# The seam between a recurrence and a dense unit: outputs split in two, products taken kind by kind, two weight sums moved

## What is computed

```python
h = rms_norm(x, norm_w) * (1 + scale) + shift          # from the conditioning vector
proj = h @ w_in                                        # 1024 x 6656
attn = sliding_window_attention(aq, ak, av, sinks) * silu(ag)
f = lb + (1 - lb) * sigmoid(rf)
rec = rms_norm(hgrn2_chunkwise(rq, f, ri), rec_norm_w) * silu(rg)
out = x + gate * (concat(attn, rec) @ w_out)
# hgrn2: b = cumsum(log f) in a chunk; q_dec = q*exp(b); k_inv = k*exp(-b)
# out = tril(q_dec k_inv^T) v  +  q_dec S      (rows' part + states' part)
# S   = decay * S + k_out^T v
```

## Time and profile before

| | us |
|---|---|
| three timed runs | 1797.95, 1798.18, 1799.14 (median 1798.18) |
| the profiled execution, its span | 1796.91, 1795.1 |
| busy PE / DVE / ACT / POOL | 1761.7 / 1284.5 / 975.0 / 476.2 |
| granted clock of PE | 0.999 of full speed |

### The profile page before, as it was taken

The page is one execution under the profiler, slowest core; times in us unless marked ns, Lnnn a source line. Parts: engine busy times, 40 slices in busy tenths (PEclk is TensorE's granted clock), DMA queues, the critical chain, the costliest instruction groups (busy, mean ns, idle before and its releaser), DMA issues.

```text
span 1795.1 us, 28444 instructions
## 1 busy us (share of the span) xinstructions
PE 1761.7 (98%) x9882; PEld 1505.8 (84%) x9882; DVE 1284.5 (72%) x2628; ACT 975.0 (54%) x2127; POOL 476.2 (27%) x825
## 2 busy tenths in 40 slices
PE   6999999999999999999999999999999999999998
PEld 4788888999978888878888899998888888888887
DVE  7965476777767676697546677776776567987986
ACT  5622224888876665562222578888655565343441
POOL 1000025777722122210002576772222220000000
PEclk9999999999999999999999999999999999999999
DMA  9242332222123354344233222121433158178242
GB/s 362 71 164 92 120 106 101 75 71 75 52 93 98 119 147 130 111 160 164 80 119 112 104 72 80 43 85 50 168 97 98 53 168 320 64 255 301 101 175 94
DMA packets 158494, 222.30 MB, mean 124 GB/s; under 512 B 11792, under 2 KB 104336, under 8 KB 150672
## 3 DMA queue, kind: packets, MB, share of 16 engines
q1 hardware_dynamic: 158352, 220.49, 36.4%
HBM read 163.18 MB, written 57.28 MB: 123 GB/s over the span
## 4 chain that ended last, share of the span: by engine, by line
PE 88%; DVE 4%; DMA 2%; ACT 2%; issue 2%; POOL 2%; SPq 0%; POOLq 0%; ACTq 0%; DVEq 0%
PE bank L924 69%; PE bank L1114 3%; PE bank L1100 3%; PE bank L1084 3%; PE bank L1209 1%; PE bank L1189 1%; PE bank L1224 1%; PE bank L1185 1%; DMA x_home<-in_x 1%; DMA h_f<-x_cols 1%; PE bank L1035 1%; PE bank L1237 1%; PE bank L1214 1%; DVE g_lo L1923 0%; ACT sm L1552 0%
## 5 line engine op out<-in xcount | busy, mean ns | idle before, releaser
L924 PE MATMUL bank<-h_hi,w_hi 128*128 128x512 f32 x512 | 206.5, 403 | 0.2
L924 PE MATMUL bank<-h_lo,w_hi 128*128 128x512 f32 x512 | 199.9, 390 | 0.0
L924 PE MATMUL bank<-h_hi,w_lo 128*128 128x512 f32 x512 | 199.7, 390 | 0.0
L924 PE MATMUL bank<-wq_hi,h_hi 128*128 128x384 f32 x512 | 179.6, 351 | 0.5 <-issue 0.5
L924 PE MATMUL bank<-ob_hi,oa_hi 128*128 128x512 f32 x448 | 175.0, 391 | 0.2 <-DVE ob_lo L2364 0.2
L924 PE MATMUL bank<-ob_hi,oa_lo 128*128 128x512 f32 x448 | 174.4, 389 | 0.0
L924 PE MATMUL bank<-ob_lo,oa_hi 128*128 128x512 f32 x448 | 174.3, 389 | 0.0
L924 PE MATMUL bank<-wq_hi,h_lo 128*128 128x384 f32 x512 | 172.1, 336 | 0.0
L924 PE MATMUL bank<-wq_lo,h_hi 128*128 128x384 f32 x512 | 171.4, 335 | 0.0
L1406 ACT ACTIVATE g_hi<-g_raw 128x2048 fp32r<-128x2048 f32 x36 | 69.0, 1916 | 162.3 <-PE bank L924 155.8
L1552 ACT ACTIVATE sm<-sm,neg_m 128x257 f32<-128x257 f32 x256 | 127.6, 501 | 6.5 <-DVE neg_m L2170 1.4
(11 more groups left out here) (258 smaller groups left out, 4670.9 us busy)
## 6 DMA issues: line engine op xcount, KB each, us to landing
g_raw<-in_w_in SPq DMA_DIRECT2D x24, 1024.0 KB, 6.1
raw<-in_w_in SPq DMA_DIRECT2D x16, 1024.0 KB, 7.9
o_lower<-mixed_cols SPq DMA_DIRECT2D x32, 512.0 KB, 6.3
nat_rows<-u SPq DMA_DIRECT2D x48, 256.0 KB, 2.6
raw<-in_w_in SPq DMA_DIRECT2D x8, 1536.0 KB, 6.7
o_upper<-in_w_out SPq DMA_DIRECT2D x24, 512.0 KB, 8.1
wa<-in_w_ada SPq DMA_DIRECT2D x8, 1024.0 KB, 11.3
g_q<-gate_cols SPq DMA_DIRECT2D x64, 128.0 KB, 2.8
```

The source lines that it names most:

```text
L924: mm = pe.matmul(dst, a, b, start=(first and m == 0), stop=(last and m == 2), **more)
```

## The change

In the last step of recurrence 0 (t = 16) PE does the rows' part of the outputs, then scores and turned keys, group 1 of product 0, and only then the states' part; group 3 of product 0 goes ahead of the transposes and outputs of step 17. ACT makes its squares behind the copy of the turned keys, and all four copies of product 0 right behind the rounding of B21, ahead of the modulation of A21. Unit 3 gets a function of its own on PE: products 1, 2, 3, 4 and 6 are issued by halves (groups 0 and 1, then 2 and 3), and in a half kind by kind over the four depths, each kind with its own wait; product 5 stays as it was. The transposes of the last rows go behind the whole of product 1. On DVE the low part of B11' (product 2) goes ahead of the last rows, and T4 goes from between the additions of product 3 to behind the combination of group 1 of product 4. SP and POOL are not edited.

```diff
+            HH, HL, LH = (0, 0), (0, 1), (1, 0)
+            def kind(n, e, which, cs, ks=range(KH), first=False, last=False):
+                at, operand = PRODUCTS[e]
+                h, w = which
+                for k in ks:
+                    for c in cs:
+                        mm = pe.matmul(ring(n, at + c)[:, :], operand(k)[h][:, tokens(c)],
+                                       (g_hi, g_lo)[w][w_slot(n, e)][:, k, :], start=(first and k == 0),
+                                       stop=(last and k == KH - 1), skip_group_check=True)
+                        if last and k == KH - 1:
+                            mm.then_inc(blk_ok, 1)
+            def by_kinds(n, e, cs):
+                at = (PRODS + 1) * (n // GU) + e + 2
+                pe.wait_ge(whi_ok, PRODS * n + e + 1)
+                pe.wait_ge(hhi_ok, at)
+                kind(n, e, HH, cs, first=(e != 1))
+                for which in ((HL, LH) if e == 2 else (LH, HL)):
+                    if which == HL:
+                        pe.wait_ge(wlo_ok, PRODS * n + e + 1)
+                    else:
+                        pe.wait_ge(hop_ok, at)
+                    kind(n, e, which, cs, last=(which == (LH if e == 2 else HL)))
+            def first_unit(n):
+                s, halves = n // GU, ((0, 1), (2, 3))
+                if s > 0:
+                    for cs in halves:
+                        pe.wait_ge(p1_ok, 4 * n + cs[1] + 1)
+                        by_kinds(n, 1, cs)
+                    mix_transposes(s - 1, REC_T - 1)
+                for cs in halves:
+                    if s > 0 and cs[0] == 0:
+                        pe.wait_ge(rmix_ok, QB * s * REC_T)
+                    elif s > 0:
+                        pe.wait_ge(ot_ok, s * REC_T)
+                    by_kinds(n, 2, cs)
+                for cs in halves:
+                    pe.wait_ge(c11_ok, 4 * n + cs[1] + 1)
+                    by_kinds(n, 3, cs)
+                for cs in halves:
+                    pe.wait_ge(comb_ok, comb(n, COMB_U2, cs[1]))
+                    by_kinds(n, 4, cs)
+                for c in range(4):
+                    pe.wait_ge(comb_ok, comb(n, COMB_22, c))
+                    strassen(n, s, 5, c)
+                for cs in halves:
+                    pe.wait_ge(comb_ok, comb(n, COMB_U3, cs[1]))
+                    by_kinds(n, 6, cs)
             def gemm_p1(s, u, c):
...
                 n = s * GU + u
+                if n in (GU,):
+                    first_unit(n)
+                    return
                 if u > 0:
...
+                output_rows(T, t)
+                output_states(T, t)
+            def output_rows(T, t):
                 b = t % 2
...
                               skip_group_check=True)
+            def output_states(T, t):
+                b = t % 2
                 pe.wait_ge(st_ok, STEPS * (T + 1))
...
                         break
+                    if t == REC_T + 1:
+                        gemm_p1(s + 1, 0, 3)
                     if t >= 3:
                         mix_transposes(s, t - 3)
-                    if t >= 2:
+                    if t == REC_T:
+                        output_rows(T - 2, t - 2)
+                    elif t >= 2:
                         outputs(T - 2, t - 2)
...
                         chunk_products(s, T - 1, t - 1)
-                    if t == REC_T and s + 1 < SEGS:
+                    if t == REC_T:
                         gemm_p1(s + 1, 0, 1)
+                        output_states(T - 2, t - 2)
                     if 1 <= t <= REC_T:
...
                         transpose_half(half)
-                    if s + 1 < SEGS and t >= REC_T - 1:
-                        gemm_p1(s + 1, 0, (0, 2, 3)[t - (REC_T - 1)])
+                    if s + 1 < SEGS and REC_T - 1 <= t <= REC_T:
+                        gemm_p1(s + 1, 0, (0, 2)[t - (REC_T - 1)])
...
                         forget_tanh(s, t)
-                    if s + 1 < SEGS and t == REC_T + 1:
-                        for c in range(3):
-                            copy_p1(s + 1, GU * (s + 1), c)
                     if t >= 3 and not (s + 1 == SEGS and t == REC_T):
                         mix_copy(s, t - 3)
-                    if s + 1 < SEGS and t == REC_T:
-                        mix_squares(s, t)
                     if t < REC_T:
...
                     if s + 1 < SEGS and t == REC_T:
+                        mix_squares(s, t)
                         hi_a12(s + 1)
                         weights_hi(GU * (s + 1), 1)
+                        for c in range(4):
+                            copy_p1(s + 1, GU * (s + 1), c)
                         modulate_a21(s + 1)
...
                         if t == REC_T + 1:
-                            copy_p1(s + 1, GU * (s + 1), 3)
                             weights_hi(GU * (s + 1), 2)
...
                 if n == GU:
+                    weights_lo(n, 2)
                     mix_rows(s - 1, REC_T + 1)
-                    weights_lo(n, 2)
                 else:
...
                 add_u2(1)
-                weights_t4(n)
+                if n not in (GU,):
+                    weights_t4(n)
                 add_u2(2)
...
                     dve.tensor_tensor(c22[c % 3][:], ring(n, 4 + c)[:, :], u3[c][:], ALU.add).then_inc(comb_ok, 1)
+                    if n in (GU,) and c == 1:
+                        weights_t4(n)
                 if u == 0:
```

## The result

The changed kernel's median is 1800.66 us (1797.51 to 1804.93, 22 runs), that of the kernel before beside it 1798.2 us (1795.81 to 1800.79, 22 runs): ratio 1.0013, 95% interval 1.0007 to 1.0019. So it is slower by 2.3 us (1.3 to 3.4), less than 0.2%. Predicted: 1799.9, within 0.2%.

The account below looks back on a forecast made before the run. PE bounds the kernel (busy 1761.7 of 1795.1 us), with DVE next. Waits closed -3.3, products 3 and 4 late +2.0, store +3.0 give +1.7 us: median 1799.9 us, range 1795.4 to 1802.6, no change within 0.2%.

Parts of the forecast that it names:

- Part 1: Recurrence 0's last step: PE's 2.7 us wait at the states' part goes; group 2 waits for the masked copy, 2.3 us earlier.
- Part 2: ACT and last rows: r_mix ready at about 787.4 instead of 785.2; product 2 starts at 787.9 against 791.20, 3.3 us gained.
- Part 3: Products 3 and 4: ACT's later meeting and DVE's chain cost 2.0 us; product 4 starts at 811.6, 1.3 us gain left.
- Part 4: T4 moved: the c22 store lands at 832.9 behind two loads; PE stalls 3.0 us before product 5's group 3.
- my own sign: Start of product 4: if it comes by 810.3, the step on products 3 and 4 being late is wrong.
- Rival (a): Product 5: the c22 store doesn't hold group 3; -1.3 us, 1796.9 us; chance 0.18.
- rival (b): Products 3 and 4: DVE's chain isn't the bound either, all 3.3 to 3.7 us are kept; 1794.7 us; chance 0.12.
- Rival (c): Product 5: the store lands later than 835 us, PE stalls 7.7 us; +6.4 us, 1804.6 us; chance 0.12.
- Rival (d): Step 16: scores wait for k_inv or the masked copy comes later; 1 to 2 us less gain, 1801.2 us; chance 0.08.

Follow-up runs that it names:

- store_first: Changed kernel with SP storing c22 of groups 0 and 1 before it waits for T4 and issues the two 1 MB loads; ratio 0.9984 to the kernel before.
- act_store: Changed kernel with the store of c22 of group 0 issued by ACT on its own DMA queue after T4; ratio 1.0011 to the kernel before.
- one_load: Changed kernel with SP issuing only one of the two loads ahead of the store of c22 of group 0; ratio 0.999 to the kernel before.
- fill_wait: Changed kernel with 12 more matmuls, results unused, on PE ahead of product 5's last group; ratio 1.0003 to the kernel before.
- t4_alone: Kernel before with only T4 moved behind the combination of group 1; ratio 1.0026 to the kernel before.
- t4_back_mask: Changed kernel with T4 in its old place and the masked copy of the scores right behind the state carries on DVE; ratio 0.9987 to the kernel before.
- kinds_only: Kernel before with unit 3 by halves and kinds and B11' low part ahead of the last rows; recurrence, ACT, T4 as before; ratio 1.0001 to before.
- t4_back: Changed kernel with T4 back in its old place between the additions of product 3; ratio 0.9983 to the kernel before.

## Why the prediction was right

The forecast (+1.7 us, no change by 0.2%, a touch slow) holds with +2.3 (1.3 to 3.4). Step by step:

- **Part 1, right in kind.** The states' part waits no more, group 2 waits for the masked copy, as named. I put 0.3 to 0.5 us; it is 0.19 us in the profiles of store_first, act_store, one_load and fill_wait, but 1.51 in the changed kernel's. There the load of rg_w for step 15 took 5.4 us to land where it was 2.8 before. DVE's scaling was held until 767.54 and the copy stands behind it. This load took 2.7 to 3.1 us in eight of the other profiles, 4.4 in t4_alone and 4.7 in t4_back_mask, and no edit lies ahead of it, so I take the late one for chance; how often it comes is not shown.
- **Part 2, one term off.** r_mix wasn't pushed back by POOL: the power started at 783.58 just ahead of S1 (783.61) and took 1.01 us, where it had taken 3.03 starting behind S1. r_mix started right behind the low part of B11', 1 us earlier after S1 than I had it. That the one behind waits stands: in kinds_only the power, 0.07 us behind S1, took 3.09 us, in the other runs it came first and took 1.01.
- **Part 3, sign right, size too big.** I had 2.0 us lost to ACT's meeting and DVE's chain. ACT did wait for the meeting, but it came 4.4 us after the last transposes (790.48 to 794.92) and not 6.0, because the last rows' store now lands in 2.9 us and not 4.4: B22's load is 2.65 us ahead of it (789.18, 791.83) instead of 1.4. The other runs agree: issued 1.4 to 1.6 us behind that load the store takes 4.1 to 4.4 us, 2.1 behind it 3.6 to 3.9, 2.65 behind it about 3.0, and 5.1 behind it 2.3 (kinds_only). With r_mix 1 us earlier too, product 4 of store_first starts at 810.20, 49.24 us after the transposes, 2.8 less than before's 52.05:

```profile
810.20 2.14 PE L970 MATMUL bank<-g_hi,h_hi 128*128 128x512 f32 x8
```

So of 3.3 us only 0.5 is lost, and by my own sign (product 4 by 810.3) the size of this step is wrong. The bound is still DVE's sum u2: t4_back's trace names it as what product 4 waits for (0.20 us). In the changed kernel's profile the late masked copy took 1.3 of the gain, and so product 4's start agreed with my sum (1.45 against 1.36 earlier) by an accident.
- **Part 4, the step that decides, right.** The store lands 9.2 us after T4 (8.3 predicted), PE's wait is 3.50 us in the trace and the group is 3.66 late (830.7 and 3.0 predicted, on my clock). store_first, t4_back and t4_alone show that nothing else carries the loss. What I gave as its cause, order within SP's ring, is only half of it: in act_store another queue didn't help.
- **Not foreseen:** the half clock behind the wait, 1.3 us in the changed kernel (4.18 us for 2.85); my sum has no term for it.

So two misses of opposite sign met: 1.5 us too much for part 3, 2.0 too little for part 4. The mechanism that decides was right, but that the time came within 0.6 us of the forecast is luck. With +0.5 for part 3 and 3.7 + 1.3 for part 4 the sum is -3.3 + 0.5 + 5.0 = +2.2 us, against the measured 2.3. Rival (a), a store that doesn't hold anything, is what store_first makes true, and the gain is then 2.9 us, nearer to rival (b) than to the 1.3 that I gave to it. Rival (c) with its 7.7 us stall didn't come: the second load took 8.0 us to land, near the 7.1 that I used and not the 12.0 of that rival. Rival (d), a masked copy that comes later still, did come in the profiled execution, at 1.3 us, and in none of the other profiles.

## What to carry to other kernels

When an operation is moved later on one engine, read the queue that waits for it: whatever stands behind that wait in the queue's order moves too, and here a 256 KB store that freed a buffer was caught behind 2 MB of loads. A small transfer that someone will wait for goes ahead of the loads on the same queue; another queue didn't save it here. And a wait closed at one place is worth little while the next engine's work isn't let in by finer waits: the split and the order kind by kind gained nothing that the time shows alone, and 2.0 us of the seam together (2.6 with T4 moved and the store first).

## What the runs showed of the hardware

- Behind PE's waits of 3.50 us (changed), 3.19 us (t4_alone) and 3.04 us (act_store) the granted clock fell to the 1.2 GHz level for some 2.8 us (about 3.3 in act_store): 0.50 in 835.8 to 838.6 of the changed kernel. In act_store it fell only 1.0 us after PE had started again, as its timeline shows (a later matmul of a row is some 0.39 us long at full clock, as in the earlier trace rows, 0.63 at the lower). Behind the 2.68 us of the kernel before it stayed at 1.00, matmuls as fast as ever.
- A store issued from ACT's queue in the same 0.1 us as the first of two 1 MB loads from SP's took 8.7 us for 256 KB. On SP's own queue it took 8.3 us behind both loads and 5.7 us between them; alone it takes 2.4.
- A power of 128x4 on POOL took 3.03 and 3.09 us when it started 0.12 and 0.07 us behind a DVE sum of 2.29 us (before, kinds_only), and 1.01 us when it started 0.03 to 0.07 us ahead of it (the ten others).

```profile
833.16 0.50 PE L924 MATMUL bank<-g_hi,s_hi 128*128 128x512 f32 x1 [3.04 <-DVE c L2155]
...
834.19 0.56 PE L924 MATMUL bank<-g_lo,s_hi 128*128 128x512 f32 x1
834.55 0.63 PE L924 MATMUL bank<-g_hi,s_lo 128*128 128x512 f32 x1
```
